# Two expert layers: blocks of 32 rows on four column strips in one stream, in place of 64-row blocks on two strips in two streams

## The reference

```python
def moe_ffn(h, w_rg, b_rg, w_re, b_re, w_gate, w_up, w_down):
    g_idx = argmax(h @ w_rg + b_rg)                  # one of 4 groups
    top_v, top_i = top_k(e_logits of that group, 2)  # two of its 8 experts
    gate = g_w * softmax(top_v)
    expert = g_idx * 8 + top_i
    # rows of h sorted by expert, padded to blocks
    def expert_block(xblk, e):
        hid = silu(xblk @ w_gate[e]) * (xblk @ w_up[e])   # 1024 -> 512
        return hid @ w_down[e]                            # 512 -> 1024
    return zeros_like(h).at[row_tok].add(yb * row_w[:, None])
```

## Time and profile before

| | |
|---|---|
| Median of 3 runs | 4325.1 us (4321.26 to 4328.98) |
| Span of the profiled execution | 4317.1 us |
| The profiled execution's own time around the span | not recorded; the median is 8.0 us over the span |
| PE busy | 3905.6 us, 90% of the span |
| DVE, ACT, POOL busy | 34%, 21%, 5% |
| Layer 0: routing, blocks | 2417 to 2464 us, 2464 to 3087 us |
| Layer 1: routing, blocks | 3595 to 3644 us, 3645 to 4247 us |
| DMA over the span, over layer 0's blocks | 152 GB/s, 374 GB/s |

### The profile page before, as it was taken

The page is one execution under the profiler, slowest core; times in us unless marked ns, Lnnn a source line. Parts: engine busy times, 40 slices in busy tenths (PEclk is TensorE's granted clock), DMA queues, the critical chain, the costliest instruction groups (busy, mean ns, idle before and its releaser), DMA issues.

```text
span 4317.1 us, 49805 instructions
## 1 busy us (share of the span) xinstructions
PE 3905.6 (90%) x19318; PEld 1952.7 (45%) x19319; DVE 1489.1 (34%) x2779; ACT 900.5 (21%) x1887; POOL 211.2 (5%) x337
## 2 busy tenths in 40 slices
PE   5997888999999889999889799989799996999995
PEld 3554665555444554444664333333344443333333
DVE  2576666413203662252563411111321124111115
ACT  3003444202001331221252211111110002111111
POOL 0000000000000000000000011110100000111101
PEclk9998999999999999999999899999899998999997
DMA  8111223101110000010340299997601103999994
GB/s 315 71 39 40 99 99 118 49 23 39 58 39 20 1 1 30 37 59 11 117 157 2 107 394 382 423 418 303 247 20 39 39 21 135 398 396 393 420 375 149
DMA packets 78975, 656.73 MB, mean 152 GB/s; under 512 B 9440, under 2 KB 11304, under 8 KB 45408
## 3 DMA queue, kind: packets, MB, share of 16 engines
q0 software_dynamic: 36992, 339.36, 19.5%
q1 hardware_dynamic: 23168, 280.66, 16.2%
q10 hardware_dynamic: 18656, 34.49, 2.2%
HBM read 599.41 MB, written 55.05 MB: 152 GB/s over the span
## 4 chain that ended last, share of the span: by engine, by line
PE 45%; DMA 10%; DVE 4%; issue 1%; ACT 1%; POOL 0%; POOLq 0%; DVEq 0%; ACTq 0%
PE banks L259 23%; PE banks L2419 12%; DMA arena<-in_w_gu 9%; PE banks L2436 5%; PE banks L1520 1%; DMA arena<-y_tok,arena 1%; DVE arena L1635 1%; PE banks L2402 1%; PE banks L2116 1%; PE banks L2426 1%; PE banks L468 1%; DMA arena<-h_tok,arena 1%; PE banks L1589 0%; PE banks L1569 0%; DVE banks L1634 0%
## 5 line engine op out<-in xcount | busy, mean ns | idle before, releaser
L259 PE MATMUL banks<-arena 128*128 128x512 f32 (+2 forms) x4544 | 1750.7, 547 | 39.0 <-ACTq L138 16.9
L259 PEld LDWEIGHTS banks<-arena 128*128 128x128 f32 x4544 | 841.5, 191 | 936.2 <-issue 885.1
L2419 PE MATMUL banks<-arena 128*64 128x512 f32 x3136 | 710.2, 610 | 58.4 <-DMA arena<-in_w_gu 56.6
L2419 PEld LDWEIGHTS banks<-arena 128*64 128x64 f32 x3136 | 230.2, 141 | 528.7 <-issue 452.2
L2436 PE MATMUL banks<-arena 128*64 128x512 f32 x1568 | 347.5, 596 | 1.5 <-issue 1.5
L1589 PE MATMUL banks<-arena 128*64 128x128 f32 x1952 | 162.1, 285 | 54.5 <-ACT arena L1602 39.3
L2436 PEld LDWEIGHTS banks<-arena 128*64 128x64 f32 x1568 | 108.5, 137 | 205.5 <-issue 205.5
L946 DVE SCALAR_TENSOR_TENSOR arena<-arena 128x1024 f32<-128x1024 f32 x240 | 195.9, 878 | 0.2 <-DVEq L138 0.2
L2494 DVE COPY arena<-banks 128x256 f32<-128x256 f32 x98 | 41.0, 419 | 394.7 <-PE banks L2426 394.7
L302 DVE SCALAR_TENSOR_TENSOR arena<-banks,arena 128x512 f32<-128x512 f32 (+1 forms) x72 | 51.9, 721 | 333.8 <-PE banks L259 333.8
L1520 PE MATMUL banks<-arena 64*128 64x256 f32 (+2 forms) x768 | 130.3, 470 | 39.2 <-ACT arena L1691 32.8
(11 more groups left out here) (356 smaller groups left out, 3169.3 us busy)
## 6 DMA issues: line engine op xcount, KB each, us to landing
arena<-in_w_gu POOLq DMA_DIRECT2D x86, 2048.0 KB, 14.0
arena<-in_w_dn POOLq DMA_DIRECT2D x43, 2048.0 KB, 11.8
arena<-in_w_gu SPq DMA_DIRECT2D x42, 2048.0 KB, 12.0
arena<-in_w_ada SPq DMA_DIRECT2D x24, 2048.0 KB, 7.3
arena<-in_w_dn SPq DMA_DIRECT2D x21, 2048.0 KB, 14.8
y_tok<-arena ACTq DMA_DIRECT2D x196, 128.0 KB
y_tok<-arena POOLq DMA_DIRECT2D x1, 16384.0 KB, 45.1
arena<-in_ab_w_ada SPq DMA_DIRECT2D x6, 2048.0 KB, 9.3
```

The source lines that it names most:

```text
L259: last = pe.matmul(self.bank_of(g, n), lhsT, rhs, start=k == 0, stop=k == KT - 1)
L2419: last = pe.matmul(bank(2 + s_)[64 * h:64 * h + 64, :], xbT[:, k, 64 * s_:64 * s_ + 64], w_gu[s_][:, k, h], start=k == 0, stop=k == KT - 1 ...
```

## The change

What it does, part by part:

- `BLK` is 32. A block's rows are gathered as four quarter rows each: 128 rows of 256 channels, so that a 128x256 tile holds one block, and two transposes turn it (`turn_x`). `w_gu` is stored in another order for this.
- Gate and up run on four column strips: each matmul takes 32 rows as weights and 128 columns of w_gate and w_up, for one of four strips (`tile_position=(0, 32 * q)`). Down likewise, with 128 columns of w_down.
- There is one stream of blocks. The experts alternate over the two slots. PE runs gate and up of expert i + 1 ahead of down of expert i (`in_turn`); the turned hid of every block is kept in `held`, which takes the whole of the weight ring.
- The order of the experts is: even places from the fewest blocks up, odd places from the most down. Experts 31 and 0 always stand first, so that their weights can be loaded before routing is known: gate and up of expert 0 from the end of the attention or convolution stage on, expert 31 from the end of the output projection on, down of expert 0 once the table is there.
- Loops over an expert's blocks run between bounds from a table (`cum`), two register loads for each loop on PE, ACT and DVE. Every expert has at least one block.
- ACT issues the weight loads, each behind the loop that frees the part. SP stores y, four transfers of 32 KB for a block, into a ring of 8. POOL only gathers, 8 ahead.
- The next stage's first two weight units go into the ring only behind `m0_blocks`, and POOL clears the block semaphores there, which both layers share.

```diff
-BLK = 64
+BLK = 32
@@ blocks_pe: one stream, gate and up ahead of down
+            def gu_half(self, pe, slot, part, j):
+                for q2 in range(4):
+                    for q in range(4):
+                        last = pe.matmul(bank(2 + part)[32 * q:32 * q + 32, 0:128],
+                                         xbT[:, 128 * j + 32 * q2:128 * j + 32 * q2 + 32], w_gu[slot][part][:, 2 * q2 + j, q],
+                                         start=j == 0 and q2 == 0, stop=j == 1 and q2 == 3, tile_position=(0, 32 * q),
+                                         skip_group_check=True)
+                return last
...
+            def in_turn(self, eng, first, second):
+
+                first(0, 0)
+                with eng.Fori(0, E // 2 - 2) as p:
+                    first(2 * p + 1, 1, p)
+                    second(2 * p, 0, p)
+                    first(2 * p + 2, 0, p + 1)
+                    second(2 * p + 1, 1, p)
+                for i in range(E - 3, E):
+                    first(i, i % 2)
+                    second(i - 1, (i - 1) % 2)
+                return
...
+                def gate_up(i, slot, nth=None):
+                    nth = i // 2 if nth is None else nth
+                    begin, end = self.cum(pe, i), self.cum(pe, i + 1)
+                    pe.wait_ge(self.wa[slot], 16 * nth + 16)
+                    pe.sem_inc(passed, 1)
+                    pe.wait_ge(self.wb[slot], 16 * nth + 16)
+                    pe.sem_inc(passed, 1)
+                    with pe.Fori(begin, end) as b1:
+                        pe.wait_ge(self.x0, b1)
+                        pe.wait_ge(self.ma, b1)
+                        self.gu_half(pe, slot, 0, 0)
+                        pe.wait_ge(self.x1, b1)
+                        self.gu_half(pe, slot, 0, 1).then_inc(self.ga, 1)
+                        pe.wait_ge(self.mb, b1)
+                        self.turn_hid(pe)
+                        pe.wait_ge(self.xr[1], b1)
+                        self.turn_x(pe).then_inc(self.xt[1], 1)
+                        self.gu_half(pe, slot, 1, 0).then_inc(self.gb0, 1)
+                        self.gu_half(pe, slot, 1, 1).then_inc(self.gb, 1)
...
+                    with pe.Fori(begin, end) as b1:
+                        pe.wait_ge(self.y0, b1)
+                        pe.wait_ge(self.h0, b1)
+                        self.dn_half(pe, slot, 0, (0, 1))
+                        pe.wait_ge(self.h1, b1)
+                        self.dn_half(pe, slot, 0, (2, 3)).then_inc(self.d0, 1)
+                        pe.wait_ge(self.y1, b1)
+                        self.dn_half(pe, slot, 1, (0, 1)).then_inc(self.dm, 1)
+                        self.dn_half(pe, slot, 1, (2, 3)).then_inc(self.d1, 1)
@@ blocks_act: silu, then the weights of the expert after next
+                def gate_up(i, slot, nth=None):
+                    with a.Fori(self.cum(a, i), self.cum(a, i + 1)) as b1:
+                        a.wait_ge(self.ga, b1)
+                        a.activation(sg[:, 0:64], bank(2)[:, 0:64], ACT.Silu).then_inc(self.sa, 1)
+                        a.wait_ge(self.gb, b1)
+                        a.activation(sg[:, 64:128], bank(3)[:, 0:64], ACT.Silu).then_inc(self.sb, 1)
+                    if nth is not None or i + 2 < E:
+                        e = self.expert(a, i + 2)
+                        for part in range(2):
+                            self.load_gu(a, slot, e, part)
@@ blocks_dve
+                def gate_up(i, slot, nth=None):
+                    with d.Fori(self.cum(d, i), self.cum(d, i + 1)) as b1:
+                        d.wait_ge(self.sb, b1)
+                        d.tensor_tensor(hid[:, 64:128], sg[:, 64:128], bank(3)[:, 64:128], ALU.mult).then_inc(self.mb, 1)
+                        self.keep_hid(d, b1)
...
+                def down(i, slot, nth=None):
+                    with d.Fori(self.cum(d, i), self.cum(d, i + 1)) as b1:
+                        at = ((b1 + 1) & (HELD - 1)) * 128
+                        d.wait_ge(self.dm, b1)
+                        d.tensor_copy(hidS[:, 0:64], held[:, bass.ds(at, 64)]).then_inc(self.h0, 1)
+                        d.wait_ge(self.d1, b1)
+                        d.tensor_copy(hidS[:, 64:128], held[:, bass.ds(at + 64, 64)]).then_inc(self.h1, 1)
@@ blocks_sp: weights before routing is known
+                sp.wait_ge(stage_end, closed(("ev_attn", "od_conv")[self.l]))
+                for part in range(2):
+                    self.load_gu(sp, 1, 0, part)
+                sp.wait_ge(stage_end, closed(("ev_out", "od_out")[self.l]))
+                for part in range(2):
+                    self.load_gu(sp, 0, E - 1, part)
+                self.load_dn(sp, 0, E - 1)
+                sp.wait_ge(m_tg, self.l + 1)
+                self.load_dn(sp, 1, 0)
```

More of the change, by code:

```diff
@@ L2245, in route_dve @@
+                link(d.tensor_scalar(key, blocks, c("key", 32)[:, 0:1], c("key", 32)[:, 1:2], ALU.mult, ALU.add))
                 d.tensor_copy(keys, key.broadcast_to([32, 32])).then_inc(m_nb, 1)
-                link(d.tensor_copy(n_blk, ends[0:32, 1:2].broadcast_to([32, 128])))
-                d.wait_ge(m_pb, 2 * l + 1)
-                d.tensor_scalar(order[:, 0], bank(7)[0:32, 65:97], key, None, ALU.is_lt)
-                d.tensor_scalar(order[:, 1], bank(7)[0:32, 65:97], key, None, ALU.is_le).then_inc(m_nb, 1)
+                d.wait_ge(m_pb, 3 * l + 1)
@@ new lines, in route_dve @@
+                link(d.tensor_scalar(place, place, 2.0, 1.0, ALU.mult, ALU.add))
+                link(d.tensor_scalar(mirror, place, -1.0, 2.0 * E - 1.0, ALU.mult, ALU.add))
+                link(d.tensor_tensor(place, place, mirror, ALU.min))
+                at = place[:, 32:33]
+                link(d.tensor_scalar(order[:, 0:32], place[:, 0:32], at, None, ALU.is_gt))
+                link(d.tensor_scalar(order[:, 32:65], c("iota", 32)[:, 0:33], at, None, ALU.is_gt))
+                link(d.tensor_copy(n_blk, blocks.broadcast_to([32, 128])))
@@ new lines, in blocks_pool @@
+                for i in range(XB):
+                    self.gather(g, i, i)
+                    if i >= 3:
+                        g.wait_ge(self.xg[(i - 3) % 4], 16 * (1 + (i - 3) // 4))
+                        g.sem_inc(self.x_ok[min(i - 3, 2)], 1)
+                top = self.cum(g, E)
+                turns = (top + 11) >> 3
+                with g.Fori(1, turns) as m:
+                    for i in range(XB):
+                        g.wait_ge(self.xr[1], 8 * m + (i - 7))
+                        g.sem_inc(passed, 1)
+                        self.gather(g, 8 * m + i, i)
+                        g.wait_ge(self.xg[(i - 3) % 4], 32 * m + 16 * (1 + (i - 3) // 4))
+                        g.sem_inc(self.x_ok[2], 1)
@@ new lines, in dn_half, with clear_pool @@
+            def dn_half(self, pe, slot, h, chs):
+                for ch in chs:
+                    for q in range(4):
+                        last = pe.matmul(bank(6 + h)[32 * q:32 * q + 32, 0:128], hidS[:, 32 * ch:32 * ch + 32],
+                                         w_dn[slot][:, ch, 256 * q + 128 * h:256 * q + 128 * h + 128], start=ch == 0,
+                                         stop=ch == 3, tile_position=(0, 32 * q), skip_group_check=True)
+                return last
+            def clear_pool(self, g):
+                for name in block_sems:
+                    g.sem_clear(block_sems[name])
```

467 lines of the change are left out of this document (196 added, 271 removed).

## The result

The changed kernel takes 4520.87 us (median of 4 runs, 4507.54 to 4525.6) against 4327.04 for the kernel before: 1.0449 times as long, 95% interval 1.0426 to 1.0471. The forecast was 4204, with a range of 4130 to 4345. It was slower where a gain was forecast. The profiled execution's span is 4519.0 us, 201.9 more than before.

The account below looks back on a forecast made before the run. It took PE and DMA to take turns as the bound in the block stages. From the span 4317.1, less 119 for the stages and 9 for routing, plus 7, gives 4196; with 8.0 around it 4204 us, range 4130 to 4345.

Parts of the forecast that it names:

- Loops and hand-overs: Block stages: 64 loop entries a layer at 0.4 us each, some 26 us a layer; DVE, ACT and SP work costed at nothing.
- The slower rival: Block stages: PE's queue no longer covers loads and trips; 1.22 us an entry, 0.6 a pass, some 4425 us; chance 0.17.
- Its argument against: Against the slower rival: PE ran through two loads and a branch in every round with no gap in the chain.
- The block: A 32-row block on PE: 192 records at 28 ns plus transposes and strip changes, 5.9 us; 478 or 466 us a layer.
- DMA: Block stages: a pair of experts takes 29.6 + 0.62 n us at 425 GB/s; the larger of PE and DMA counts.
- The end: End of each block stage, from the last down to the last store landed, four stores on SP: 5 us.
- Around the stages: Outside the block stages: routing 9 us less in all, 7 us more behind layer 0's blocks for semaphore clearing and late loads.
- routing's gain: Routing loses some forty small DVE ops and one PE trip, gains six, a trip and a wider table: 4.5 us less each.
- Instruction fetch: Rival: PE's larger loop body no longer fits, 14 returns a layer wait for packets; 4260 us at 2 us each; chance 0.04.
- 81 ns a matmul: The skill's figure for 128 columns, not taken: a block would be 15.6 us and the kernel some 1400 us slower.
- signs of being wrong: PE gaps over 0.7 us at every loop pass, records at 33 ns or more, instruction packets throughout, DMA share under 0.85.
- Padding: Block stages: nothing won per row in ideal records; the win is less padding, 81 half blocks for 100.

Follow-up runs that it names:

- more_loads: The changed kernel with one more, unused, loop-bound load per entry, on DVE ahead of down and on PE ahead of gate and up: 4666.69 us, ratio 1.0781.
- hoist: The changed kernel with the four bounds of an expert-loop pass loaded once at its top on PE, ACT and DVE, replacing eight loads: 4461.77 us, ratio 1.0316.
- light1: The changed kernel with each weight transfer that ACT issues in layer 1 bringing only the first eighth of its unit: 4519.67 us, ratio 1.0441.
- early_4stores: carry_4stores with DVE copying the turned hid for down earlier, so that no copy stands between PE's two loops: 4366.38 us, ratio 1.0094.
- carry_4stores: The changed kernel with bounds loaded once a pass, two kept in registers from the pass before, and the wait for all stores on ACT: 4380.43 us, ratio 1.0134.

## Why the prediction was wrong

- **Loops and hand-overs: the step that failed.** It took 0.4 us for a loop entry, "since PE's queue ran through the two loads of every round unseen". Measured: 63 gaps, most of 1.5 to 2.3 us, 131 and 124 us a layer where 26 were taken; one load is 0.65 us (more_loads), and taking loads away brought 59 us (hoist). POOL's 2.44 us for four loads and two entries held this price all along: 0.61 a load. I split it over entries and took a third of it, for cover that was not there. The way into down hangs on DVE's sequencer, which stands behind DVE's own last copy. On the way out PE's queue covers too little, and the old kernel's trace shows what the cover had been: PE's sequencer reached the branch (L2408) and the two loads (L2409) of a new round while the down records, 7.02 us from 2983.70 on the earlier trace rows, still ran to 2990.72, so it was 4.4 us ahead of them. The changed kernel's sequencer reaches the end of a down loop (L2434) with the records 2643.53 to 2645.48, 0.9 us ahead, and its second load (L2290) starts when they are over. Before, then now (PEldq is PE's sequencer; ns min/median/max, first and last start in us):

```profile
L2408 PEldq ALU_OP  x1: 32/32/32, 2986.3 to 2986.3; - x1
L2409 PEldq TENSOR_LOAD <-arena x2: 299/299/299, 2986.8 to 2987.5; - x2
```

```profile
L2434 PEldq ALU_OP  x1: 36/36/36, 2644.6 to 2644.6; - x1
L2290 PEldq TENSOR_LOAD <-arena x2: 297/303/309, 2644.9 to 2645.7; - x2
```

- **The slower rival** had the mechanism and the sign, but a price of 4425 and a chance of 0.17. Its per-pass cost (0.6) was too high, its per-entry cost (1.22) too low: it priced two loads (1.3 us) and not the last copies, the semaphore trips and the branch beside them. It named the copy of hid ("copied only behind the last gate and up") and gave it no price. Its argument against, that the chain showed no gap in a round, is the same mistake.
- **The block.** Records stand 26.5 ns apart (1.95 less about 0.25 for the last one, over 64), so 28 was right within 6%, and the trace's 26.2 better. But a block took 6.3 us of PE and 0.3 of gaps, for 5.9: 34 and 26 us in layer 0. What was missing is this last one's 0.25 us, which comes again wherever the stream of records breaks, and the breaks themselves: in each down block (DVE's copy of hid comes 0.23 us late) and, in some sets, in nearly each gate and up block.
- **DMA.** The larger of PE and DMA was taken for each pair of experts, and DMA was the larger in twelve of layer 0's sixteen. With stages of 713 us it was so only once, 6.9 us for in_w_gu in layer 0, and an eighth of the bytes changed nothing in layer 1 (light1).
- **The end** was to cost 5 us; it cost 18 and 15: SP's backlog of stores and POOL's 7.25 us of drain, which the old program, where ACT waited for the stores, did not have on the path. SP's four issues for a block were counted as if free, because they are off PE.
- **The clock** was not in the sum: 19 and 41 us of records at half clock behind gaps of 2 to 3 us.
- **Around the stages** it was nearly right. From the out projection's last long run of matmuls to the first row gather it is 160.3 us for 161.9 in layer 0 and 166.1 for 165.9 in layer 1, where 4.5 less each was forecast; behind layer 0's blocks it is 3.2 more (395.6 for 392.4) where 7 were. Of routing's gain only 1.6 us came, in layer 0. Chain of the changed kernel, then of before, for those starting points:

```profile
2301.31 68.93 PE banks L258 x160
...
3570.61 70.47 PE banks L258 x160
```

```profile
2302.82 68.93 PE banks L259 x160
...
3479.01 71.09 PE banks L259 x160
```

- **Instruction fetch** did not come: the instruction queue brought 132 packets over the span for 113, and none from 2520 to 3070 us, in the loops of layer 0. The Trainium skill, "Runtime: NRT & Kernel Launch", section "Instruction fetch mechanics", gives PE 128 KiB, in which the prediction's estimated 53 KB fit; the trace agrees.
- **81 ns a matmul,** which the Trainium skill, "TensorE: Matmul & The Clock Gate", section "Back-to-back issue gap", gives for 128 columns, does not hold for this kernel's shape: on four column strips records stand 26.5 ns apart, on each strip one in four. The prediction was right not to take it. Whether it holds for matmuls on the whole array no reading here tells.
- **Signs.** Of the prediction's signs of being wrong a DMA share under 0.85 came (0.74 over the stage); gaps of over 0.7 us came, released by DVE, but at every change of loop and not at every pass.
- **Padding.** The forecast's source of gain is real but small: 81 blocks at 4.6 + 2.2 us are 551 us of PE for 560 in 25 rounds. Whatever is added at a hand-over is more.

## What to carry to other kernels

Price a loop entry by its register loads, on the engine that comes last at that entry (here DVE on the way into down, PE on the way out): each was 0.65 us here, and what hid it was work already queued on the critical engine. Smaller blocks leave less queued: PE's sequencer was 4.4 us ahead of its records at the old loads and 0.9 us at the new. Load bounds once, carry them in registers, and let no copy for the next loop depend on the last instruction of this one: together with the moved wait this took 154 us off the changed kernel on one chip, of which the copy was the smallest part, 14. And compare versions on one chip: an edit seemed to bring 50 us until both versions ran side by side.

## What the runs showed that I had not expected

- One kernel differed by 40 to 60 us between sets on different chips (4465 to 4509; 4316 to 4378) while the kernel before, in the same sets, stayed within 3 us. It goes with a gap of 0.2 to 0.35 us in a long run of 128-column records, at no wait. What makes it, on the chip or around it, stays open. Placing the loop's head did not remove it; announcing the back edge ran only in a set without the gap and tells nothing.
- One more register load at each hand-over, 75 us of waiting, cost 146 us: with PE's gaps near 3 us the granted clock fell from 0.97 to 0.90. Fewer gaps did not bring it back in turn: with 67 us of gaps less, early_4stores was granted 0.96 where carry_4stores had 0.98.
- POOL's drain took 7.25 us when it stood behind the wait for the stores, and nothing of the path when ACT waited in its place.
- SP waited up to 23 us for a store of 128 rows of 1 KB to land beside the weight loads, and up to 7 for four stores of 32 rows.
